# A streaming encoder on one core: the squares of the new residual added in pairs on GpSimd before TensorE sums them

## The reference, cut to what matters

```python
def rmsnorm(x, g):
    y = xf * lax.rsqrt(jnp.mean(xf * xf, axis=-1, keepdims=True) + RMS_EPS)
    return (y * g.astype(jnp.float32)).astype(x.dtype)

def residual_update(x, h_m, attn, w_out, g_post_mix, g_pre_ffn, w_ffn_in, w_ffn_out, g_post_ffn):
    x = x + rmsnorm(jnp.concatenate([h_m, attn], axis=-1) @ w_out, g_post_mix)
    h = rmsnorm(x, g_pre_ffn)
    gate, up = jnp.split(h @ w_ffn_in, 2, axis=-1)
    return x + rmsnorm((jax.nn.silu(gate) * up) @ w_ffn_out, g_post_ffn)
```

## Time and profile before

| | |
|---|---|
| Median of 3 runs | 2938.61 us (2929.41 to 2940.33) |
| The profiled execution, its own time | 2939.65 us |
| Its span | 2937.8 us |
| TensorE (PE) busy | 2871.6 us, 98% |
| VectorE (DVE) busy | 1608.8 us, 55% |
| ScalarE (ACT) busy | 985.9 us, 34% |
| GpSimd (POOL) busy | 1482.6 us, 50% |
| Mean granted clock of TensorE | 0.989 |

### The profile page before, as it was taken

How to read it: one execution, slowest core, us unless ns; L and a number is a source line. 1 busy time by engine, 2 the same in 40 slices (tenths; PEclk the granted TensorE clock), 3 DMA queues, 4 the chain that set the end, 5 groups by cost and what they waited for, 6 DMA issues and landing times.

```text
span 2937.8 us, 45844 instructions
## 1 busy us (share of the span) xinstructions
PE 2871.6 (98%) x17057; PEld 2660.4 (91%) x17057; DVE 1608.8 (55%) x2161; ACT 985.9 (34%) x1926; POOL 1482.6 (50%) x1186
## 2 busy tenths in 40 slices
PE   8999999999999999999899999999999999999998
PEld 7999967779999999999789998677889999999997
DVE  7433345644765555655783333456457655655566
ACT  4222234432233333333341223244332333333333
POOL 2223242234367888887422222332333788888782
PEclk9999989999999999999999999799999999999999
DMA  5121210021211111111322112100212111111113
GB/s 167 42 41 33 38 39 1 1 88 51 84 41 50 50 57 43 57 43 43 110 88 54 31 31 38 31 1 1 95 44 95 44 43 57 43 57 43 52 48 133
DMA packets 211566, 154.92 MB, mean 53 GB/s; under 512 B 40856, under 2 KB 195112, under 8 KB 210672
## 3 DMA queue, kind: packets, MB, share of 16 engines
q1 hardware_dynamic: 194304, 111.29, 14.3%
q10 hardware_dynamic: 17136, 41.89, 3.8%
HBM read 128.56 MB, written 24.59 MB: 52 GB/s over the span
## 4 chain that ended last, share of the span: by engine, by line
PE 32%; issue 24%; POOLq 23%; POOL 13%; DVE 5%; ACT 2%; DVEq 1%; ACTq 0%; DMA 0%
PE acc L776 7%; PE acc L780 7%; PE acc L779 7%; POOL slab_lo L692 5%; POOLq L709 3%; POOLq L704 3%; POOLq L699 3%; POOL slab_raw L710 2%; POOLq L713 2%; POOLq L719 2%; POOLq L716 2%; POOL small_lo L692 2%; POOLq L722 2%; POOLq L655 1%; DVE residual L2161 1%
## 5 line engine op out<-in xcount | busy, mean ns | idle before, releaser
L557 POOL TENSOR_TENSOR slab_hi<-slab_raw,ones 128x1024 fp32r<-128x1024 f32 x63 | 123.5, 1961 | 680.5 <-PE acc L776 514.0
L692 POOL TENSOR_TENSOR slab_lo<-slab_raw,slab_hi 128x512 fp32r<-128x512 f32 (+1 forms) x376 | 414.2, 1110 | 101.9 <-ACT slab_hi L1948 66.4
L776 PE MATMUL acc<-act_hi,slab_hi 128*128 128x352 f32 x1296 | 426.6, 329 | 8.2 <-ACT residual L1672 5.2
L780 PE MATMUL acc<-act_lo,slab_hi 128*128 128x352 f32 x1296 | 416.4, 321 | 0.0
L779 PE MATMUL acc<-act_hi,slab_lo 128*128 128x352 f32 x1296 | 415.7, 321 | 0.0
L1948 ACT ACTIVATE slab_hi<-slab_raw 128x512 fp32r<-128x512 f32 (+1 forms) x372 | 193.4, 544 | 394.6 <-DMA slab_raw<-in_w_ffn_in 153.0
L1330 PE MATMUL acc<-act_hi,slab_hi 128*128 128x352 f32 x992 | 322.1, 325 | 0.9 <-ACT small_lo_f L1980 0.5
L1333 PE MATMUL acc<-act_hi,slab_lo 128*128 128x352 f32 x992 | 318.2, 321 | 0.0
L1334 PE MATMUL acc<-act_lo,slab_hi 128*128 128x352 f32 x992 | 317.8, 320 | 0.0
L2737 DVE TENSOR_TENSOR branch<-acc,branch 128x704 f32<-128x704 f32 x288 | 256.7, 891 | 88.3 <-PE acc L1398 74.0
L692 POOL TENSOR_TENSOR small_lo<-slab_raw,small_hi 128x256 fp32r<-128x256 f32 (+1 forms) x224 | 217.7, 976 | 115.2 <-ACT small_hi L1948 79.8
(11 more groups left out here) (511 smaller groups left out, 7349.7 us busy)
## 6 DMA issues: line engine op xcount, KB each, us to landing
slab_raw<-in_w_ffn_in SPq DMA_DIRECT2D x152, 256.0 KB, 2.9
slab_raw<-in_w_in SPq DMA_DIRECT2D x40, 512.0 KB, 3.9
slab_raw<-in_w_ffn_out SPq DMA_DIRECT2D x80, 256.0 KB, 2.5
x_spill<-residual ACTq DMA_DIRECT2D x2, 4224.0 KB, 12.4
residual<-x_spill ACTq DMA_DIRECT2D x2, 4224.0 KB, 14.1
f_spill<-residual ACTq DMA_DIRECT2D x2, 4224.0 KB, 11.5
slab_raw<-in_w_out SPq DMA_DIRECT2D x16, 512.0 KB, 4.5
slab_raw<-in_w_ffn_in SPq DMA_DIRECT2D x12, 512.0 KB, 3.7
```

The source lines that it names most:

```text
L557: pool.tensor_tensor(hi, raw, ONES[:, 0:1].broadcast_to([P, SLAB]), ALU.mult)
L692: pool.tensor_tensor(lo, QUAD[q][:, c0:c1], hi, ALU.subtract).then_inc(unit_ready, 1)
L776: mm = pe.matmul(out, wh, HH[:, x], start=k == 0, stop=False)
L780: mm = pe.matmul(out, wh, HL[:, x], start=False, stop=k == KT - 1)
```

## The change

The squares are still made in pairs of tiles by ScalarE. GpSimd, in a new function `add_pairs`, adds the second tile of each pair to the first in place, 12 additions of 128x352 at each boundary, 36 in all. TensorE's `new_x_squares` then waits for these sums and makes 4 f32 matmuls per group in place of 8, so 36 in place of 72. A second semaphore was needed for this; the kernel makes room for it by letting `oc_hi` count what `oc_lo` counted, at an unrelated place.

```diff
@@ -571,6 +572,14 @@
+            def add_pairs(z):
+
+
+                for n in range(NG):
+                    for j in range(KT // 2):
+                        pool.wait_ge(x_sq, ((z - 1) * 3 + n) * 4 + j + 1)
+                        pool.tensor_tensor(part(SQX, 2 * j, n), part(SQX, 2 * j, n), part(SQX, 2 * j + 1, n), ALU.add).then_inc(x_sq_added, 1)
+
@@ -590,6 +599,8 @@
                     key_split(l)
                     pool.wait_ge(ss_added, l)
                     split(l, 0, 0, gate_raw_landed, (l + 1) * 16 * 5)
+                if l:
+                    add_pairs(2 * l)
                 pool.wait_ge(h_part, 2 * l * 12 + 12)
@@ -684,6 +695,8 @@
                 for i, (to, use) in enumerate(FFN_PLAIN):
                     slot = i % 2
                     plain_split(l, slot, (u0, u1)[slot] + i // 2, 2 - slot, to, use)
+                    if i == 2:
+                        add_pairs(2 * l + 1)
@@ -791,11 +804,10 @@
                 for j in range(j0, j1):
-                    pe.wait_ge(x_sq, ((z - 1) * 3 + n) * 4 + j + 1)
+                    pe.wait_ge(x_sq_added, ((z - 1) * 3 + n) * 4 + j + 1)
                     if j == 0:
                         pe.wait_ge(pre_rs, (z - 1) * 3 + n)
-                    for k in (2 * j, 2 * j + 1):
-                        mm = pe.matmul(bank(7, TG), ONES[:, :], part(SQX, k, n), start=k == 0, stop=k == KT - 1)
+                    mm = pe.matmul(bank(7, TG), ONES[:, :], part(SQX, 2 * j, n), start=j == 0, stop=j == KT // 2 - 1)
@@ -1193,8 +1205,7 @@
-                pe.wait_ge(oc_hi, l + 1)
-                pe.wait_ge(oc_lo, l + 1)
+                pe.wait_ge(oc_hi, 2 * l + 2)
@@ -2504,8 +2515,8 @@
-                dve.wait_ge(oc_hi, l + 1)
-                dve.tensor_tensor(OCL[:, :], bank(7, 512), OCH[:, :], ALU.subtract).then_inc(oc_lo, 1)
+                dve.wait_ge(oc_hi, 2 * l + 1)
+                dve.tensor_tensor(OCL[:, :], bank(7, 512), OCH[:, :], ALU.subtract).then_inc(oc_hi, 1)
```

More of the change, by code:

```diff
@@ L358, in encoder_step @@
         ss_turned, pt_first, pt_second = sem("sample_turned"), sem("sample_pt_first"), sem("sample_pt_second")
-        ss_mixed, oc_hi, oc_lo, ss_wide, attn_out = sem("sample_mixed"), sem("sample_oc_hi"), sem("sample_oc_lo"), sem("sample_wide"), sem("attn_out")
+        ss_mixed, oc_hi, ss_wide, attn_out = sem("sample_mixed"), sem("sample_oc_hi_then_lo"), sem("sample_wide"), sem("attn_out")
+        x_sq_added = sem("x_square_pairs_added")
         mix_hi, mix_ready = sem("mix_hi"), sem("mix_ready")
```

## The result

| | before | after |
|---|---|---|
| Median of 7 runs each, same chip | 2933.45 us (2921.3 to 2940.33) | 2956.62 us (2942.63 to 2964.88) |
| The profiled execution, its span | 2939.65, 2937.8 us | 2964.34, 2962.5 us |
| Mean granted clock of TensorE | 0.989 | 0.981 |

The ratio is 1.0077, 95% interval 1.0051 to 1.0104: slower by about 0.8% where 0.66% was forecast, and the median lies inside the range.

The account below looks back on a forecast made before the run. The prediction took the three boundaries to be VectorE chains with TensorE's sums beside them. Collisions of 6.8 + 5.3 + 6.8 = +18.9 us gave 2958.6 from the profiled 2939.65 us, or 2957.5 from the median: 2958 us, range 2947 to 2968.

Parts of the forecast that it names:

- VectorE's chain sets the boundaries, and TensorE's saving is worth nothing: Three boundaries: TensorE's sums lie beside VectorE's chain, so 22 us saved becomes waiting; rival that it counts, 0.05.
- The additions shut VectorE out: Boundaries: a GpSimd addition reading SBUF makes VectorE instructions with two SBUF inputs wait; +18.9 us in all.
- 0.62 us a collision: Boundaries: each 0.945 us addition beside VectorE costs it 0.66 of its time; rival of less than half the total, 0.19.
- The prediction's other form: Boundaries: a collision costs the addition's 0.945 us less a fixed part (1.29 - 1.10), 0.755 us.
- The whole-instruction reading of the rule: Boundaries: each collision costs VectorE the whole 0.945 us addition, 28.8 us in all, 2967 us; rival's chance 0.08.
- Where they fall: First and third boundary: eleven of twelve additions collide, 6.8 us each; group 0's pair 3 falls in VectorE's wait.
- The longer path to the sum is hidden: Group ends: square, addition and one matmul take 2.4 us, covered by VectorE's 2.9 us to its low part.
- The second boundary, 5.3 us: Second boundary: collisions of about 0.9 us in group 0, 1.9 in group 1 and 2.5 in group 2.
- The clock does not fall: Starts of the next products: no loss from TensorE's clock; rival that it falls adds 4.9 us, 2963 us, chance 0.12.
- The sum: All three boundaries: 6.8 + 5.3 + 6.8 = +18.9 us, with nothing against it.
- TensorE idle 40 us more: Boundaries: TensorE's idle time up some 40 us, the 22 saved and the 19 added.

Follow-up runs that it names:

- e2_no_adds: Kernel before, with TensorE summing only the even tiles, four matmuls a group, and no GpSimd additions; median 2936.58 us, ratio 1.0014 to the kernel before.
- e7_root_first: Kernel before, with ScalarE's root for group 1 moved ahead of group 0's last square; median 2927.52 us, ratio 0.9986 to the kernel before.
- e4: Changed kernel with only pairs 0 and 2 added on GpSimd, the others summed as before, six matmuls a group; median 2943.19 us, ratio 1.0028 to before.
- e6: Changed kernel with each GpSimd addition made twice, first into a spare place, then in place; median 2974.44 us, ratio 1.0151 to the kernel before.
- e1: Changed kernel with additions written to a spare place and TensorE summing all eight tiles behind them; median 2955.89 us, ratio 1.0060 to the kernel before.
- e3: Changed kernel with each addition replaced by a GpSimd memset of about equal length, even tiles alone summed; median 2934.79 us, ratio 1.0008 to before.
- e9: Changed kernel with each addition replaced by a GpSimd copy of one tile, even tiles alone summed; median 2944.66 us, ratio 1.0023 to before.
- e5_keep_busy: Changed kernel with six extra small TensorE matmuls behind each of group 2's first three sums; median 2954.42 us, ratio 1.0065 to the kernel before.
- e8: Kernel before with the root moved as in e7_root_first and even tiles alone summed, no additions; median 2932.38 us, ratio 1.0013 to the kernel before.
- e10: Kernel before with the root moved as in e7_root_first and two high parts ahead of the branch's third root on ScalarE; 2926.31 us, ratio 0.9982.

## Why the prediction was right, step by step

- **VectorE's chain sets the boundaries, and TensorE's saving is worth nothing**: right. e2_no_adds takes 36 matmuls away at no price and gains nothing. The cover was thinner than the earlier trace rows made it seem, as e7_root_first shows: 1.6 us less on VectorE brings the sums onto the path.
- **The additions shut VectorE out**: right, and shown from several sides: by the number of them (e4, e6), without their use (e1), with a GpSimd that is busy but does not read (e3), and with one that reads once (e9). The Trainium skill, page "SBUF — State Buffer", section "SBUF: two separate sides", says that a VectorE instruction with two SBUF inputs is shut out only by a GpSimd instruction that reads SBUF. This case agrees: the fill of 0.96 us costs nothing and the copy of 0.48 us costs 0.24.
- **0.62 us a collision**: right in size, 7.05 / 11 = 0.64. It was got as a share of the addition, 0.66 x 0.945, and that form was wrong. The prediction's other form, GpSimd's duration less a fixed part (0.755), came nearer: what counts is how far GpSimd's instruction still has to run when VectorE's starts, less 0.15 us. That the share gives nearly the same number for an addition that starts 0.16 us ahead is luck; in e1_adds_aside, with a lead of 0.07 us, it is 0.71, and for the copy it is half, not two thirds. The whole-instruction reading of the rule of the Trainium skill's page "SBUF — State Buffer", as the prediction put it, would give 0.93 a collision. In these rows VectorE starts after the addition has begun (717.18 and 717.02), so that it could lose at most 0.77; it lost 0.62.
- **Where they fall**: eleven at each outer boundary, right. That they would spread over scalings and sums was mostly wrong: nearly each addition met the next sum, or the four scalings of normed. A pair's own scalings were met in one place of the outer boundaries, at 2186.33.
- **The longer path to the sum is hidden**: right. At the first boundary VectorE's low part ends at 754.81, 0.09 us behind the last sum of squares (753.18 + 1.54), which the lower clock had lengthened.
- **The second boundary, 5.3 us**: it was 5.95. The collisions alone came to 4.6 and not 5.3, since the additions of group 0 met one sum and not the start of group 1, and one of group 1 cost 0.22. The splits cost 0.7 us more by other timing, and a wait behind TensorE at the lower clock cost 0.67. That the parts nearly made up for each other is luck.
- **The clock does not fall**: this failed. I gave the fall 0.12 and argued that TensorE would never be without a matmul for 4.4 us (the wait in question, 1457.48 to 1462.43, is 4.95 us in the trace). In group 2 of the outer boundaries it was without one for at most 1.85 us in a row, and the clock fell all the same. It cost 1.8 us at each outer boundary, 3.55 in all. At the second the release came at the low clock too, but from the first low part of group 1 to the third copy both kernels take 20.0 us, so nothing was lost behind the release; 0.67 us were lost ahead of it, in the chain, as shown above. There TensorE did stand for 3.45 us, and earlier for 7.01 (4.95 before). e5_keep_busy gives the 1.8 us back and leaves the rest, which ties the loss at the outer boundaries to the thin sums.
- **The sum**: 6.8 + 5.3 + 6.8 = 18.9 predicted; 7.05 + 5.95 + 7.00 = 20.0 measured, and 3.55 for the clock behind it, a term that I had put at nothing. Against the profiled executions I was 5.8 us low (2958.6 against 2964.3). That the median, 2956.6, comes within 1.4 us of my 2958 is luck: the three runs that I started from had a median 5.2 us above the 2933.45 of the seven, and that hid the missing clock. In the difference, +18.9 stands against +23.2.
- **TensorE idle 40 us more**: wrong. Span less busy goes from 66.2 to 89.1 us, 22.9 more. A lone sum takes 0.86 us, or 1.54 at the low clock, not the 0.61 of a row of eight: all the sums together take 34.2 us where they took 46.5, 12 less and not 22. Other matmuls at the low clock, those at the start of the next product among them, took that back and more.

## What to carry to other kernels

A busy share of 98% says nothing of a boundary: look at who releases the first instruction after it, and take the work away without paying for it (as e2_no_adds) before building anything that pays. Work moved to GpSimd is free for VectorE only if it doesn't read SBUF while VectorE reads two operands from it; count the collisions, and price each by what is left of GpSimd's instruction when VectorE's starts, less some 0.15 us. And a TensorE that is relieved between short waits may start the next product at half clock, so leave it the work, or give it some.

## What the runs showed of the hardware that was not expected

**A GpSimd fill is invisible to VectorE**: one of 0.96 us that runs beside a two-operand sum costs it 0.00 us. An addition of 0.93 us costs 0.62.

**The clock falls with short waits.** TensorE had 0.86 us of work in each 2.57 us (747.90 to 750.47), and its clock went to 0.50; with 1.45 us in each 2.65 us (e1_adds_aside) it stayed at 1.00. The longest wait alone doesn't decide: in e3_fill the clock fell at the end of the first boundary with no wait over 1.10 us, in e4_half_adds it held with one of 1.51. The six kernels that make four sums a group with nothing between them (changed, e2, e3, e6, e8, e9) have a start of 16.0 to 17.7 us in all twelve places, the other six one of 15.2 to 15.4.

**Behind one and the same wait it falls in most executions, not in all, and not at the same moment.** One wait of 2.63 us for VectorE's small_lo, between the first and second boundary, stands in all twelve traces, in a part that no edit touches. In two of them (before and e7) the matmuls behind it take 0.32 us after a first one of 0.40. In the other ten, 8 to 19 matmuls take 0.49 or 0.50: from the start of the work in the changed kernel, and only from the seventh matmul on in e10. The changed kernel's stretch reads

```profile
1438.00:1440.00 2.00, 1.94 (x7) 1.97 (x8) 1.22 (x3) 0.63 (x1) 0.57 (x1) 0.50 0.00 0
```

The spread between runs goes with the clock. In 77 runs of the kernel before, taken beside the experiments, the mean granted clock ran from 0.985 (2948.2 us) to 0.997 (2917.7 to 2920.5 us), about 2.3 us for each 0.001; the seven of the changed kernel ran from 0.990 (2942.63 us) to 0.981 (2964.88 us). A change of 2 or 3 us is read from distances between instructions, not from medians. What decides whether and when the clock falls behind a given wait was not settled.
